# Expert outputs in a mixture-of-experts step: written by lane, or scattered in token order with empty lanes skipped

## The reference

```python
g_idx = argmax(x @ router_group_w + b)              # one of 4 groups
top_v, top_i = top_k(logits of that group, 2)       # two of its 4 experts
gates = one_hot(...) * softmax(top_v) * g_w         # 16 columns, two not zero
hid = silu(x @ w_gate[e]) * (x @ w_up[e])           # 16 experts, 1024 -> 256
out = sum over e of gates[t, e] * (hid @ w_down[e]) # 256 -> 1024
y = rms_norm(x + g2 * out) * final_norm
```

## Time and profile before

| | us |
|---|---|
| median of three runs (706.13 to 708.97) | 707.57 |
| the profiled execution | 713.57 |
| its span, first to last instruction | 711.6 |
| PE / DVE / ACT / POOL busy in the span | 608.3 / 531.0 / 338.2 / 132.6 |
| expert stage and what follows it | from about 484 to the end |

### The profile page before, as it was taken

One profiled execution on the slowest core, in us unless ns is written; L12 is line 12 of the kernel. 1 busy time (PEld: TensorE's weight loads), 2 busy tenths in 40 slices (PEclk: granted clock), 3 DMA queues, 4 the chain that ended last, 5 costly groups with the idle time before them and its releaser, 6 DMA issues.

```text
span 711.6 us, 8242 instructions
## 1 busy us (share of the span) xinstructions
PE 608.3 (85%) x3212; PEld 485.7 (68%) x3212; DVE 531.0 (75%) x667; ACT 338.2 (48%) x447; POOL 132.6 (19%) x86
## 2 busy tenths in 40 slices
PE   0889999999999979999799999926999999999420
PEld 0369778899888656555578888815888878788310
DVE  0583599999999767998863610897999888887467
ACT  5142124331113745556645211454588877886452
POOL 0002000006993000000222432002112111102240
PEclk9889999999999979999999999965999999999765
DMA  7973858965002100000344300098799999997673
GB/s 270 412 262 117 323 178 317 370 210 203 2 3 84 59 1 0 1 0 1 120 167 161 127 1 1 21 388 292 309 401 422 419 418 420 420 420 279 233 289 147
DMA packets 45488, 147.07 MB, mean 207 GB/s; under 512 B 7297, under 2 KB 16101, under 8 KB 37769
## 3 DMA queue, kind: packets, MB, share of 16 engines
q1 hardware_dynamic: 35112, 116.25, 42.7%
q0 software_dynamic: 5472, 20.45, 7.4%
q10 hardware_dynamic: 4864, 9.84, 3.6%
HBM read 126.44 MB, written 20.09 MB: 206 GB/s over the span
## 4 chain that ended last, share of the span: by engine, by line
PE 44%; DVE 30%; DMA 16%; ACT 4%; issue 4%; ACTq 1%; POOLq 0%; SPq 0%; DVEq 0%; POOL 0%
DVE cy L1464 9%; PE ps L564 7%; PE ps L566 7%; PE ps L565 7%; DMA m_raw<-in_moe_w_gate_dram 6%; DMA raw<-in_w_ada_dram 4%; PE ps L728 3%; DMA m_raw<-in_moe_w_down_dram 2%; PE ps L865 2%; PE ps L868 2%; PE ps L867 2%; DVE w_lo L1422 2%; PE ps L546 2%; DVE ss_qk L1579 1%; DVE gu_lo L1874 1%
## 5 line engine op out<-in xcount | busy, mean ns | idle before, releaser
L1464 DVE SCALAR_TENSOR_TENSOR cy<-cu,tapw,cy 128x655 f32<-128x655 f32 x120 | 114.7, 956 | 3.5
L1874 DVE TENSOR_TENSOR gu_lo<-m_raw,gu_hi 128x2048 fp32r<-128x2048 f32 x36 | 82.3, 2290 | 18.3 <-ACT gu_hi L1194 18.2
L1194 ACT ACTIVATE gu_hi<-m_raw 128x2048 fp32r<-128x2048 f32 x36 | 68.8, 1915 | 23.8 <-DMA m_raw<-in_moe_w_gate_dram 14.5
L865 PE MATMUL ps<-gu_hi,xt_h 128*128 128x512 f32 x144 | 60.4, 419 | 8.4 <-DVE gu_lo L1874 8.4
L564 PE MATMUL ps<-w_hi,mix 128*128 128x512 f32 x160 | 62.8, 392 | 2.8 <-DVE w_lo L1661 2.8
L867 PEld LDWEIGHTS ps<-gu_lo,xt_h 128*128 128x128 f32 x288 | 56.3, 195 | 12.7
L1351 POOL TENSOR_TENSOR w_lo<-raw,w_hi 128x2048 fp32r<-128x2048 f32 x7 | 32.7, 4678 | 167.4 <-ACT w_hi L1122 167.4
L566 PE MATMUL ps<-w_hi,mix 128*128 128x512 f32 x160 | 62.3, 389 | 0.0
L565 PE MATMUL ps<-w_lo,mix 128*128 128x512 f32 x160 | 62.3, 389 | 0.0
L868 PE MATMUL ps<-gu_hi,xt_l 128*128 128x512 f32 x144 | 58.4, 405 | 0.0
L867 PE MATMUL ps<-gu_lo,xt_h 128*128 128x256 f32 x288 | 58.4, 285 | 0.0
(11 more groups left out here) (346 smaller groups left out, 1434.3 us busy)
## 6 DMA issues: line engine op xcount, KB each, us to landing
raw<-in_w_ada_dram SPq DMA_DIRECT2D x24, 1024.0 KB, 8.1
m_raw<-in_moe_w_gate_dram SPq DMA_DIRECT2D x18, 1024.0 KB, 10.1
m_raw<-in_moe_w_up_dram SPq DMA_DIRECT2D x18, 1024.0 KB, 13.2
m_raw<-in_moe_w_down_dram SPq DMA_DIRECT2D x18, 1024.0 KB, 14.7
raw<-in_w_in_dram SPq DMA_DIRECT2D x11, 1024.0 KB, 8.3
y_rows<-ys ACTq DMA_DIRECT2D x17, 512.0 KB, 8.7
raw<-in_w_out_dram SPq DMA_DIRECT2D x8, 1024.0 KB, 5.5
y_rows<-pool_u POOLq DMA_DIRECT2D x1, 5120.0 KB, 27.4
```

What stands on the lines that cost most here:

```text
L865: pe.matmul(out, xt_h[q][:, k, :], gu_hi[q][:, k, :], start=(k == 0), stop=False)
L1194: act.activation(gu_hi[q][:, :, u * FF:(u + 1) * FF], m_raw[3 * s + u][:, :].rearrange("p (k n) -> p k n", k=KB), ACT.Copy).then_inc((g_hi ...
L1464: ins = dve.scalar_tensor_tensor(out=cy[:, blk, :], in0=cu[:, blk, i:i + CY], scalar=w, in1=cy[:, blk, :], op0=MUL, op1=ADD)
L1874: dve.tensor_tensor(gu_lo[s][u][:, :, :], m_raw[3 * s + u][:, :].rearrange("p (k n) -> p k n", k=KB), gu_hi[q][:, :, u * FF:(u + 1) * FF]. ...
```

## The change

- `y_rows` becomes a table of 1280 rows in token order: row `token` for a token's first expert, `640 + token` for its second. `h2_rows` has 640 rows. Both fills with zeros and the waits for them are gone.
- A second list, `dest`, says for each lane of each block to which row of `y_rows` it goes. It is made with the overflow part of `idx`: `token_list(1, ...)` has 40 columns (`N_LIST1`) and not 12, and `late_lists` turns both into integers behind `hidden(0)`, not ahead of block 5. `posf` and `slots` are gone.
- POOL scatters `ys` by `dest` (`scatter`), four blocks behind its gathers. ACT no longer starts a DMA in the loop. Gathers and scatters carry a bounds check that is no error: a lane whose number lies beyond the table is skipped. So `xg` is set to zero once before the first gather.
- The gather of block NE+1 is ahead of the overflow loop; a turn of the loop gathers block r+NE+2 and scatters block r+NE.
- Overflow blocks and block NE keep the low part of down in set 2 (`down_slot`). So SP may load the next raw down weights when `down_lo` is done, not `down`.
- At the end SP reads `ya[t]` and `yb[t]` with ten plain DMAs, as each block's rows are contiguous. DVE scales `ya[0]`; ACT scales the others.

The diff, without declarations of semaphores and small tiles (a line "..." stands for what is left out):

```diff
@@ -195,9 +197,11 @@
     xg = [at(f"xg{q}", [D], L + 12288 + 4096 * q) for q in range(2)]
+    xg_both = at("xg_both", [2 * D], L + 12288)
+    dest = at("dest", [NTILE + 2], L + 40704, i32)
...
     tile_hot = at("tile_hot", [2, TT, NTILE + 2], L + 25600)
-    tile_row = [at("tile_row0", [2, TT, NE], L + 26720, f32r), at("tile_row1", [2, TT, NTILE + 2 - NE], L + 27360, f32r)]
+    tile_row = [at("tile_row0", [2, TT, NE], L + 26720, f32r), at("tile_row1", [2, TT, N_LIST1], L + 27360, f32r)]
@@ -343,6 +346,10 @@
         return i % 2 if isinstance(i, int) else 0
+    def down_slot(i):
+        return SETS - 1 if not isinstance(i, int) or i == NE else raw_set(i)
@@ -497,15 +504,19 @@
             sp.dma_start(g2t[:, cnd, :], row[cnd, 3].partition_broadcast(P)).then_inc(g1_in, 16)
...
             load_weights(sp, e, NE % SETS, 1)
-            sp.wait_ge(dn_ps, r + (NE + 1))
+            sp.wait_ge(dl_made, r + (NE + 1))
...
         sp.wait_ge(y_sent[0], extra * 16 + 16 * Q1)
+        for t in range(TT):
+            for a, y in ((0, ya), (1, yb)):
+                sp.dma_start(y[t][:, :], y_rows[a * TOK + t * P:a * TOK + (t + 1) * P, :]).then_inc(ya_in[t], 16)
@@ -879,7 +889,7 @@
-            q, s = hi_set(i), raw_set(i)
+            q, s = hi_set(i), down_slot(i)
@@ -891,7 +901,7 @@
         tokens(0, 0, 16)
-        token_list(1, 5, NTILE + 2 - NE)
+        token_list(1, 5, N_LIST1)
@@ -952,8 +962,6 @@
         for j, (k0, nk, col, cols, what, blk0) in enumerate(W_IN):
-            if what == "pool" and blk0 == 0:
-                act.wait_ge(zlist_in, 32)
@@ -1235,9 +1243,6 @@
             act.activation(ys[q][:, :], pair(3, D), ACT.Copy).then_inc(ys_made, 1)
-            act.wait_ge(ys_made, i + 1)
-            at_i = slice(i, i + 1) if isinstance(i, int) else bass.ds(i, 1)
-            act.dma_start(y_slots[:, at_i, :].rearrange("p a n -> p (a n)"), ys[q][:, :]).then_inc(y_sent[q], 16)
@@ -1267,6 +1272,8 @@
+        act.wait_ge(gates_made, 1)
@@ -1303,11 +1309,7 @@
         pool.memset(pool_u[:, :, :], 0.0).then_inc(cleared, 1)
-        pool.wait_ge(hi_made, 6)
         pool.wait_ge(cleared, 2)
-        zeros = pool_u[:, :, :].rearrange("p g n -> p (g n)")[:, 0:D]
-        pool.dma_start(h2_rows[TOK:TOK + P, :], zeros).then_inc(zlist_in, 16)
-        pool.dma_start(y_slots[:, NE:NTILE, :], zeros.unsqueeze(1).broadcast_to([P, N_OV, D])).then_inc(zlist_in, 16)
@@ -1351,36 +1353,52 @@
         def gather(i):
-            pool.indirect_dma_start(xg[i % 2][:, :], None, h2_rows, bass.IndirectOffsetOnAxis(ap=idx[:, i:i + 1], axis=0)).then_inc(xg_in[i % 2], 16)
-        pool.wait_ge(zlist_in, 32)
+            pool.indirect_dma_start(xg[i % 2 if i <= NE else 0][:, :], None, h2_rows, bass.IndirectOffsetOnAxis(ap=idx[:, i:i + 1], axis=0),
+                                    bounds_check=TOK - 1, oob_is_err=False).then_inc(xg_in[i % 2 if i <= NE else 0], 16)
+        def scatter(i):
+            pool.wait_ge(ys_made, i + 1)
+            pool.indirect_dma_start(y_rows, bass.IndirectOffsetOnAxis(ap=dest[:, i:i + 1], axis=0), ys[i % 2][:, :], None,
+                                    bounds_check=2 * TOK - 1, oob_is_err=False).then_inc(y_sent[i % 2], 16)
+        pool.wait_ge(h2_gain, TT)
+        pool.memset(xg_both[:, :], 0.0).then_inc(xg_clear, 1)
+        pool.wait_ge(xg_clear, 1)
...
                 pool.wait_ge(xt_ps, i - 1)
-            if i == NE:
+            gather(i)
+            if i == 4:
                 pool.wait_ge(idx_made, 2)
-            gather(i)
+            if i >= 4:
+                scatter(i - 4)
+        pool.wait_ge(xt_ps, NE + 1)
+        gather(NE + 1)
+        for i in range(NE - 3, NE):
+            scatter(i)
...
         with pool.Fori(0, extra) as r:
-            pool.wait_ge(xt_ps, r + (NE + 1))
+            pool.wait_ge(xt_ps, r + (NE + 2))
             pool.tensor_tensor(ahead[:, 6:7], zero_i[:, 0:1], zero_i[:, 0:1], ADD)
-            pool.tensor_copy(idxc[1][:, :], idx[:, bass.ds(r + (NE + 1), 1)]).then_inc(idxc_made, 1)
+            pool.tensor_copy(idxc[1][:, :], idx[:, bass.ds(r + (NE + 2), 1)]).then_inc(idxc_made, 1)
...
             pool.tensor_tensor(ahead[:, 7:8], zero_i[:, 0:1], zero_i[:, 0:1], ADD)
-            pool.indirect_dma_start(xg[0][:, :], None, h2_rows, bass.IndirectOffsetOnAxis(ap=idxc[1][:, 0:1], axis=0)).then_inc(xg_in[0], 16)
-        pool.wait_ge(slots_made, 1)
-        pool.wait_ge(y_sent[1], 16 * Q1)
-        pool.wait_ge(y_sent[0], extra * 16 + 16 * Q1)
-        pool.tensor_tensor(idxc[0][:, :], idx[:, 0:1], idx[:, 0:1], ADD).then_inc(idxc_made, 1)
-        for t in range(TT):
-            for a, y in ((0, ya), (1, yb)):
-                pool.indirect_dma_start(y[t][:, :], None, y_rows, bass.IndirectOffsetOnAxis(ap=slots[:, a, t:t + 1], axis=0)).then_inc(ya_in[t], 16)
+            pool.indirect_dma_start(xg[0][:, :], None, h2_rows, bass.IndirectOffsetOnAxis(ap=idxc[1][:, 0:1], axis=0),
+                                    bounds_check=TOK - 1, oob_is_err=False).then_inc(xg_in[0], 16)
+            pool.wait_ge(ys_made, r + (NE + 1))
+            pool.tensor_tensor(ahead[:, 5:6], zero_i[:, 0:1], zero_i[:, 0:1], ADD)
+            pool.tensor_copy(idxc[0][:, :], dest[:, bass.ds(r + NE, 1)]).then_inc(destc_made, 1)
+            pool.wait_ge(destc_made, r + 1)
+            pool.tensor_tensor(ahead[:, 3:4], zero_i[:, 0:1], zero_i[:, 0:1], ADD)
+            pool.indirect_dma_start(y_rows, bass.IndirectOffsetOnAxis(ap=idxc[0][:, 0:1], axis=0), ys[0][:, :], None,
+                                    bounds_check=2 * TOK - 1, oob_is_err=False).then_inc(y_sent[0], 16)
+        pool.wait_ge(xg_in[0], extra * 16 + 16 * (Q1 + 2))
+        pool.tensor_tensor(ahead[:, 4:5], zero_i[:, 0:1], zero_i[:, 0:1], ADD)
@@ -1805,16 +1823,19 @@
-        def hot_of(part, which, a, b):
-            hot = tile_hot[:, :, :, a:b].rearrange("p a t n -> p (a t) n")
-            link(dve.tensor_tensor(hot, iota[:, a:b].unsqueeze(1).broadcast_to([P, 2 * TT, b - a]),
+        def tiles_hot(which, a, b):
+            link(dve.tensor_tensor(tile_hot[:, :, :, a:b].rearrange("p a t n -> p (a t) n"), iota[:, a:b].unsqueeze(1).broadcast_to([P, 2 * TT, b - a]),
                                    flat_of(which).unsqueeze(2).broadcast_to([P, 2 * TT, b - a]), ALU.is_equal))
-            return dve.tensor_tensor(tile_row[part][:, :, :, :].rearrange("p a t n -> p (a t) n"), hot, flat_of(row_no).unsqueeze(2).broadcast_to([P, 2 * TT, b - a]), MUL)
+        def rows_times(part, col, a, b, row):
+            return dve.tensor_tensor(tile_row[part][:, :, :, col:col + b - a].rearrange("p a t n -> p (a t) n"),
+                                     tile_hot[:, :, :, a:b].rearrange("p a t n -> p (a t) n"), flat_of(row).unsqueeze(2).broadcast_to([P, 2 * TT, b - a]), MUL)
...
         dve.wait_ge(iota_in, 16)
-        hot_of(0, tile, 0, NE)
+        tiles_hot(tile, 0, NE)
+        rows_times(0, 0, 0, NE, row_no)
@@ -1839,10 +1860,14 @@
             link(dve.tensor_reduce(at_ov[:, :, :], of12[:, :, :, :], AX.X, ADD))
+            dve.tensor_scalar(to_row[:, 0, :], row_no[:, 0, :], float(-TOK), None, ADD)
+            dve.tensor_copy(to_row[:, 1, :], row_no[:, 1, :])
...
             link(dve.tensor_tensor(tile[:, :, :], tile[:, :, :], at_e[:, :, :], ADD))
-            hot_of(1, tile, NE, NTILE + 2).then_inc(hot_made, 1)
+            tiles_hot(tile, NE, NTILE + 2)
+            rows_times(1, 0, NE, NTILE + 2, row_no)
+            rows_times(1, NTILE + 2 - NE, 0, NTILE + 2, to_row).then_inc(hot_made, 1)
@@ -1853,9 +1878,12 @@
-        def slot_numbers():
+        def late_lists():
             dve.wait_ge(idx_ps, 2)
-            dve.tensor_scalar(idx[:, NE:NTILE + 1], bank(5, 0, NTILE + 1 - NE), rt[:, R_TRASH:R_TRASH + 1], None, ADD).then_inc(idx_made, 1)
+            dve.tensor_scalar(dest[:, :], bank(5, NTILE + 2 - NE, N_LIST1), rt[:, R_TRASH:R_TRASH + 1], float(TOK), ADD, ADD)
+            dve.tensor_scalar(idx[:, NE:NTILE + 2], bank(5, 0, NTILE + 2 - NE), rt[:, R_TRASH:R_TRASH + 1], None, ADD).then_inc(idx_made, 1)
+        def slot_gates():
@@ -1863,9 +1891,7 @@
             link(dve.tensor_tensor(gates[:, 0, :], rden2[:, :], gw[:, :], MUL))
-            dve.tensor_tensor(gates[:, 1, :], gates[:, 0, :], pe2[:, :], MUL)
-            link(dve.scalar_tensor_tensor(out=posf[:, :, :], in0=lane[:, :, :], scalar=float(NTILE), in1=tile[:, :, :], op0=MUL, op1=ADD))
-            dve.tensor_copy(slots[:, :, :], posf[:, :, :]).then_inc(slots_made, 1)
+            dve.tensor_tensor(gates[:, 1, :], gates[:, 0, :], pe2[:, :], MUL).then_inc(gates_made, 1)
@@ -1893,7 +1919,9 @@
             dve.wait_ge(dh_made, i + 1)
-            dve.tensor_tensor(d_lo[s][:, :, :].rearrange("p f n -> p (f n)"), m_raw[3 * s + 2][:, :],
+            if down_slot(i) != s:
+                dve.wait_ge(dn_ps, NE - 1 if isinstance(i, int) else i)
+            dve.tensor_tensor(d_lo[down_slot(i)][:, :, :].rearrange("p f n -> p (f n)"), m_raw[3 * s + 2][:, :],
```

(32 more changed lines are left out.)

1 line of the change is left out of this document (removed).

## The result

The changed kernel has a median of 707.75 us (22 runs, 703.37 to 711.68), the kernel before 709.84 on the same chip (22 runs, 706.13 to 714.56). The ratio is 0.9962, 95% interval 0.9945 to 0.9978: 2.7 us faster (1.6 to 3.9). In another round the changed kernel gave 0.9953 (0.9927 to 0.9978). Forecast were 5.05 us less and 702.5; the time lies above the range of 697.5 to 706.0. Of the 5.25 us between forecast and time, 2.3 are the base, whose median was 707.57 over three runs and 709.84 over 22; the other 3.0 are gain that did not come (5.05 forecast, 2.1 between the medians).

What follows compares the result with a forecast made beforehand. It took PE's pace to bound the first blocks, full DMA engines the later ones, and a chain of waits, then DVE, the end. +0.2 - 0.5 - 4.75 = -5.05 us from 707.57 gave 702.5; range 697.5 to 706.0, own range 701 to 704.

Steps and rivals of the forecast that it cites:

- The zero fills: Early fills of 5120 and 512 KB: removing them was worth 0, bounds 0 and -1 us, since no load was late.
- Before the first expert: Ahead of the expert stage: the token list growing from 12 to 40 columns costs +0.2 us, between 0 and +0.9.
- The loop: who moves what: Expert loop: stores moved from ACT to POOL and list work moved to block 0 make nobody wait longer; 0.
- rival 3: Expert loop: GpSimd's queue, with two indirect DMAs per block, sets the pace and makes it slower; 714.7 at 5.3 us each; chance 0.07.
- The skipped lanes: Expert loop: empty lanes move no rows; bounds 0 and -4.3 us, taken as -0.5 in all.
- owned blocks: Expert loop: each DMA engine owns blocks of lanes, so only high lanes' engines rest and the 4.3 us isn't gained.
- overflow gather: Overflow block's gather in the bound stretch: nine live lanes instead of a full 512 KB gather of 1.25 us; -0.5 us.
- rival 1: Expert loop: lanes dealt one by one relieve all engines, second stretch at PE's 9.42; -4.3 for -0.5, 698.7 us; chance 0.30.
- The end: After the last block: output block 1 combined from 680.35 instead of 685.11, all behind it following; -4.75 us, -2.6 if block 0 is late.
- ACT's shift: At the end: without two store starts, ACT, the weight split, PE's unused product and its activation come 1.0 us earlier.
- Rival 2: At the end: POOL's small operations are held while DVE works, so the end gives only 2.0 us; 705.3 us; chance 0.16.
- Sum: Whole kernel: +0.2 - 0.5 - 4.75 = -5.05 us, applied to a median of 707.57, giving 702.5.

Runs made afterwards that it cites:

- a_fill: Changed kernel with the early fill of 5120 KB of zeros put back, to rows nobody reads: ratio 0.9957 to the kernel before.
- a_full: Changed kernel without skipping: empty lanes gather rows of zeros and scatter to spare rows, 128 rows each time; ratio 0.9977 to the kernel before.
- a_full_spread: a_full with ranks dealt to partitions by the table of a_spread, every lane still moving its row: ratio 0.9961 to the kernel before.
- a_half: Changed kernel with ranks going alternately to partition p and 64 + p, empty lanes still skipped: ratio 0.9868 to the kernel before.
- a_spread: Changed kernel with ranks dealt to partitions by a constant table that spreads live lanes over all sixteen DMA engines: 701.23 us, ratio 0.9863.

## Why the prediction was wrong, step by step
- **The zero fills, 0.** Right (`a_fill`, for the large one).
- **Before the first expert, +0.2.** The 40-column list took 1.95 us where the 12-column one took 1.93: 0. Small, and the wrong nearest row: columns did not set it.
- **The loop: who moves what, "nobody waits longer", 0.** Right for POOL, with 0.97 to 2.35 us a scatter and 0.99 to 1.26 a gather, some 2.5 of 9.42; rival 3, the slow one, is refuted by its own row. (The longest indirect DMA of the trace before, the read of `ya` at 671.77, took 2.83 us, not 2.55.) `a_full` and `a_full_spread`, which skip nothing, have 136.51 and 136.29 us against 136.19 and 135.99. Of that +0.1 to +0.5 the profiles can't tell much.
- **The skipped lanes, owned blocks, and -0.5 for the overflow gather.** The choice was right: the deal is by blocks, and rival 1's relief did not come. The argument for it was not: "every deal but one gives that" is false. By pairs, or by fours in one round, the fullest engine of the changed kernel would have had 5.6 or 6.9 rows, and `a_half` ran at 9.42 with 6.8. No row of before told the deals apart, so as far as the rows go the choice was luck. The size is the failed step. As the prediction put it, "the load lands when the fullest one ends", and it took for granted that the fullest would do in the same time what it did before. They took 10.2 to 10.3 us a block, where skipping nothing takes 9.97 and the kernel before 9.9. That is +0.7 to +1.7 for -0.5, and the prediction's bounds for this part, 0 and -4.3, left out that a skipped transfer could cost. No row of before showed an uneven load, so an end above zero should have stayed in. Why the uneven load costs this is open. The overflow gather's -0.5 can't be seen apart from it.
- **Rival 1**, -4.3 to PE's 9.42 throughout, is what `a_spread` does to the hundredth: fourteen blocks in 131.88, and 9.7 us less by the ratio. The mechanism was priced rightly; its condition, live lanes evenly over the engines, is one table away.
- **The end, -4.75.** Right: -5.1 and -5.4. Block 0 was in SBUF by 672.5 where 671 to 677.5 was given, 673.5 likeliest, in a span whose last `ys` was 1.5 us earlier; block 1 follows ACT's scaling. DVE's scaling took 0.75 us and not 1.3, in the cover of the wait. ACT's shift was there. Rival 2's held operations were not: DVE's splits of the unused weights begin at 664.32, when the scatter (1.01 us from 663.69) had started. That a scatter would never be held is not borne out: the one at 512.98 took 2.35 us, beside DVE's split of 2.28 us from 512.17. So this was a matter of timing.
- **Sum.** The stages give -4.0 (0, +1.2, -5.2), the medians -2.7 (1.6 to 3.9). The rest is within what the start of the expert stage scatters and the intervals allow. The own range of 701 to 704 stood on a base from three runs, and was narrower than the base itself is known: the kernel before had medians of 709.84 to 712.3 on the chips of this study.

## What to carry to other kernels
Where transfers are the bound, ask what the fullest DMA engine moves, not how many bytes there are. Rows that are left out helped here only when the rows that stayed were dealt evenly enough over the engines, so deal live lanes in steps through the engines' groups of partitions; that cost a constant table here. And when a wait's length is forecast from "the same work on the same engine", keep an end of the range on the other side unless a row shows the new pattern.
